# Output weights multiplied by their gates on GpSimd, adaLN products moved ahead of the first QKV, split input wait, sign-turned attention scores

## The chip, the cores and the metric

One core of one Trainium2 chip runs the whole program in one launch. The metric is the device time in microseconds, as the median of runs; lower is better. TensorE (PE) multiplies matrices into eight PSUM banks, VectorE (DVE), ScalarE (ACT) and GpSimd (POOL) do the elementwise work, and DMA queues fed by SyncE (SP) and GpSimd bring the weights from HBM. The engines run their own instruction streams and meet at semaphores.

## The reference

The input is x of 256 rows and 1024 columns, in float32. A first block (gated delta net and dilated attention, then a gated FFN, then a norm) is followed by a second block of two layers. What is changed lies in that second block and at the very start:

```python
for i in range(2):
    mod = silu(c) @ ada_w[i] + ada_b[i]
    sh1, sc1, g1, sh2, sc2, g2 = split(mod, 6)
    h = rms_norm(x, norm_mix_g[i]) * (1.0 + sc1) + sh1
    y = (diff_attention, chunked_attention)[i](h, ...)   # ends in  o @ w_o
    x = x + g1 * y
    h = rms_norm(x, norm_ffn_g[i]) * (1.0 + sc2) + sh2
    x = x + g2 * grouped_moe(h, ...)                     # 16 experts, top 2
```

Both attentions add a bias to the scores and take a softmax: `s = q @ k + bias`, `p = exp(s - max(s))`. The gate g1 is one number for each of the 1024 columns of x, so `g1 * (o @ w_o)` is also `o @ (w_o * g1)`.

## The kernel before

**Products.** A float32 product is made of three fast ones: each weight unit of 128x1024 is split by ScalarE into a high part (`split_hi`, L592) and by VectorE into the rest (`split_lo`, L596), and the activations likewise (`turn_hi`, `turn_lo`, `shift_hi`, `shift_dve`). Raw units come by SyncE into a ring of six (`wraw`), 512 KB each; a slot is free for the next load when VectorE has split it. Units are numbered through the program: QKV of layer l from `U_QKV[l]`, 24 of them, and the output weights w_o from `U_WO[l]`, 8. The w_o units have split buffers of their own (`wtail`, three deep).

**Stages.** The input norm waits for all of x, then QKV, attention and delta net of the first block, the FFN (22 steps of three units), and for each layer of the second block: norm, turn (transposes on TensorE that apply the row's norm factor), QKV in six column groups, attention, output projection (`square`), norm with the router, and the MoE of eight expert pairs, 12 loads of 1 MB each.

**Adaptive modulation.** The vectors `mod` come from 48 bundles of weights (1 MB each, GpSimd's DMA queue, `load_ada`), each used in four narrow TensorE products (`ada_bundle`, L542). `ADA_PLACE` says into which free buffer a bundle is loaded, `ADA_QKV` how many bundles are done after each unit of the first QKV. `ada(n)` makes TensorE do the bundles up to n. Eight bundles (40 to 47) are left for the first QKV. GpSimd spreads the gate rows over the partitions into `mrow` (`mod_spread`).

**Filler.** `busy(bank, n)` (L1176) makes n products that nobody reads. It is called before the turn ahead of each QKV (`BUSY_MOD`, 11), after each output projection (`BUSY_WO`, 8), and in the router (15 and 6).

**Attention.** For each head (and each of two maps in layer 0) VectorE adds the bias to the scores in PSUM and takes the largest (L1021, L1023), then writes its negative (L1026), and ScalarE exponentiates with that as bias (L980).

**End of the output projection.** `add_gated` (L2767, L2770) multiplies each of the four PSUM banks by the gate into hn and adds that to x. TensorE transposes x in four banks (L775); VectorE copies banks 0 and 1 (L2897), ScalarE banks 2 and 3 (L2448) for the router's products (L2176), and VectorE copies their strips (L2901). The FFN's output is added without a gate (`add_to_x`, L2756).

**GpSimd's other work here.** It masks the bias (L1789) once the bias rows have come, and in layer 0 sums squares of the first six heads (L1798, L1800, L1802).

## Time and profile before

| | us |
|---|---|
| median of 3 runs | 1170.31 |
| lowest, highest | 1169.86, 1174.2 |
| the profiled execution | 1173.19 |
| its span on the core | 1171.4 |

The page gives the busy share of each engine, then the span in 40 slices with TensorE's granted clock and the DMA rate. The chain of waits goes back from the last instruction to what released each step. A timeline row has the start, the duration, the engine and line, output and inputs, and in brackets the idle time before it and who ended it. All durations below are of the one profiled execution.

### The profile page before, as it was taken

The numbers are of one execution on the slowest core, as the hardware profiler recorded it, in microseconds if no ns is written. First come the engines' busy times: TensorE is split into PE (matmuls) and PEld (weight loads), VectorE is DVE, ScalarE is ACT, GpSimd is POOL, SyncE is SP. The second block draws the span as 40 slices with busy tenths as digits, with TensorE's granted clock in tenths as the row PEclk, the third lists the DMA queues.
The fourth block names the chain that finished last, engine by engine and source line by source line (L and its number), as shares of the span: only waits on it lengthen the run. The fifth ranks groups of instructions, "written<-read, shape, count | busy, mean of one in ns | idle before, by whom it ended". The sixth has DMA issues, their size and how long they took to land.

```text
span 1171.4 us, 17269 instructions
## 1 busy us (share of the span) xinstructions
PE 1101.8 (94%) x6800; PEld 742.4 (63%) x6800; DVE 611.2 (52%) x1198; ACT 425.5 (36%) x733; POOL 94.9 (8%) x189
## 2 busy tenths in 40 slices
PE   6999899999999999989999999888999999999986
PEld 6887567899999877777634434227878754343422
DVE  3488756767878666586323233226757522332223
ACT  5445433644545454474411102005547421110100
POOL 0211123010211111030000000002000000000000
PEclk9999999999999999999999999998999999999999
DMA  9987694997999858744799999996576669999996
GB/s 278 298 243 274 221 323 138 265 328 221 344 337 284 274 194 309 253 181 170 283 411 410 408 409 409 409 402 204 175 260 234 248 258 409 409 409 409 410 409 252
DMA packets 164719, 356.15 MB, mean 304 GB/s; under 512 B 10648, under 2 KB 79512, under 8 KB 164512
## 3 DMA queue, kind: packets, MB, share of 16 engines
q1 hardware_dynamic: 147600, 295.81, 69.7%
q0 software_dynamic: 17024, 59.26, 14.7%
q8 instruction: 51, 0.84, 0.3%
q14 instruction: 28, 0.23, 0.0%
q10 hardware_dynamic: 16, 0.02, 0.0%
HBM read 351.89 MB, written 7.36 MB: 307 GB/s over the span
## 4 chain that ended last, share of the span: by engine, by line
PE 71%; DMA 14%; DVE 9%; ACT 3%; issue 1%; SPq 1%; POOL 0%; DVEq 0%; ACTq 0%; POOLq 0%
PE bank L606 38%; PE bank L1199 12%; DMA work<-in_moe_w_up 6%; PE bank L1209 6%; DMA ering<-in_moe_w_up 3%; DMA ering<-in_moe_w_gate 3%; PE bank L1168 2%; PE bank L542 2%; PE bank L773 2%; DMA ering<-in_ada_w 1%; DVE wlo L596 1%; PE bank L907 1%; SPq L1700 1%; PE bank L1969 1%; PE bank L1176 1%
## 5 line engine op out<-in xcount | busy, mean ns | idle before, releaser
L596 DVE TENSOR_TENSOR wlo<-wraw,whi 128x1024 fp32r<-128x1024 f32 x150 | 179.0, 1220 | 59.2 <-ACT whi L592 58.7
L592 ACT ACTIVATE whi<-wraw 128x1024 fp32r<-128x1024 f32 x150 | 153.8, 1052 | 56.9 <-PE bank L606 52.7
L606 PE MATMUL bank<-a_hi,whi 128*128 128x256 f32 x512 | 146.2, 286 | 0.3 <-DVE wlo L596 0.3
L606 PE MATMUL bank<-a_lo,whi 128*128 128x256 f32 x512 | 144.8, 283 | 0.0
L606 PE MATMUL bank<-a_hi,wlo 128*128 128x256 f32 x512 | 144.8, 283 | 0.0
L1199 PE MATMUL bank<-ering,work 128*64 128x512 f32 x576 | 129.6, 595 | 9.4 <-DMA ering<-in_moe_w_up 5.0
L1446 DVE TENSOR_TENSOR work<-work,bank 128x512 f32<-128x512 f32 x16 | 11.0, 687 | 205.3 <-PE bank L1199 205.3
L1335 ACT ACTIVATE o_hi<-work 128x512 fp32r<-128x512 f32 x32 | 20.2, 631 | 235.6 <-DVE work L1395 235.3
L606 PE MATMUL bank<-whi,a_hi 128*128 128x512 f32 x256 | 103.9, 406 | 0.8 <-DVE wlo L596 0.8
L606 PEld LDWEIGHTS bank<-a_hi,whi 128*128 128x128 f32 x512 | 98.1, 192 | 9.1 <-issue 7.0
L1199 PEld LDWEIGHTS bank<-ering,work 128*64 128x64 f32 x576 | 40.1, 137 | 96.8 <-issue 77.4
L606 PE MATMUL bank<-whi,a_lo 128*128 128x512 f32 x256 | 99.9, 390 | 0.0
L606 PE MATMUL bank<-wlo,a_hi 128*128 128x512 f32 x256 | 99.9, 390 | 0.0
L606 PEld LDWEIGHTS bank<-a_lo,whi 128*128 128x128 f32 x512 | 98.1, 192 | 0.7
L606 PEld LDWEIGHTS bank<-a_hi,wlo 128*128 128x128 f32 x512 | 98.1, 192 | 0.0
L1395 DVE SCALAR_TENSOR_TENSOR work<-bank,sm,mrow 128x512 f32<-128x512 f32 x32 | 22.7, 747 | 87.6 <-PE bank L1209 87.6
L1209 PE MATMUL bank<-ering,work 128*64 128x512 f32 x288 | 64.2, 595 | 1.1 <-DVE work L1449 1.1
L606 PEld LDWEIGHTS bank<-whi,a_hi 128*128 128x128 f32 x256 | 48.1, 188 | 17.2 <-issue 5.6
L1323 ACT ACTIVATE work<-bank,mcol 128x256 f32<-128x256 f32 x64 | 31.6, 561 | 67.0 <-PE bank L1168 67.0
L606 PEld LDWEIGHTS bank<-whi,a_lo 128*128 128x128 f32 x256 | 48.1, 188 | 10.3
L606 PEld LDWEIGHTS bank<-wlo,a_hi 128*128 128x128 f32 x256 | 48.2, 188 | 9.0 <-issue 0.2
L1199 PE MATMUL bank<-work 128*64 128x512 f32 x192 | 44.3, 596 | 3.7 <-DMA work<-in_moe_w_up 3.7
(332 smaller groups left out, 1877.2 us busy)
## 6 DMA issues: line engine op xcount, KB each, us to landing
ering<-in_moe_w_up SPq DMA_DIRECT2D x36, 1024.0 KB, 18.1
ering<-in_moe_w_down SPq DMA_DIRECT2D x36, 1024.0 KB, 18.1
ering<-in_moe_w_gate SPq DMA_DIRECT2D x36, 1024.0 KB, 17.2
work<-in_ada_w POOLq DMA_DIRECT2D x46, 512.0 KB, 7.0
ering<-in_ada_w POOLq DMA_DIRECT2D x38, 512.0 KB, 5.2
wraw<-in_w_in SPq DMA_DIRECT2D x28, 512.0 KB, 7.0
wraw<-in_a_w_qkv SPq DMA_DIRECT2D x24, 512.0 KB, 5.0
work<-in_moe_w_down SPq DMA_DIRECT2D x12, 1024.0 KB, 18.7
```

The lines of the kernel that those rows point to most:

```text
L542: mm = nc.tensor.matmul(psum[ADA_BANK[g]][32 * q:32 * q + 32, :], silc[:, k, :], ada_part(n, q // 2)[:, (q % 2) * HALF:(q % 2 + 1) * HALF] ...
L592: nc.scalar.activation(w_hi(c), wraw[:, c % RING, :], ACT.Copy).then_inc(w_hi_done, 1)
L596: nc.vector.tensor_tensor(w_lo(u[0]), wraw[:, u[0] % RING, :], w_hi(u[0]).bitcast(F32), ALU.subtract).then_inc(w_lo_done, 1)
L606: mm = nc.tensor.matmul(out_ap, l, r, start=first and n == 0, stop=last and n == len(terms) - 1)
L773: tr = nc.tensor.matmul(dst, v, hn[:, t, 0:P], start=True, stop=True)
L907: mm = nc.tensor.matmul(bank[:, t * P:t * P + (t + 1) * P], q, k, start=True, stop=True)
L1168: mm = nc.tensor.matmul(bank[:, kk * S:kk * S + cols], part[:, t, pair_cols(2 * b + kk)], sel[:, t, 0:cols // PAIR_SLOTS, :], start=n == 1 ...
L1199: mm = nc.tensor.matmul(bank[rows, :], x_e[:, k, rows], eunit(r, e)[:, kk * HALF:(kk + 1) * HALF], start=first and kk == 0, stop=last and ...
L1209: mm = nc.tensor.matmul(psum[4 + half][rows, :], hid_t[:, m % 4, rows], eunit(r, e)[:, half * HALF:(half + 1) * HALF], start=first, stop=last)
L1323: ins = nc.scalar.activation(xe[:, :, k, :], gather_bank(g, b)[:, kk * S:(kk + 1) * S].rearrange("p (a c) -> p a c", a=2), ACT.Identity, b ...
L1335: nc.scalar.activation(o_hi[:, cols], o_f[:, cols], ACT.Copy).then_inc(e_o_hi, 1)
L1395: return nc.vector.scalar_tensor_tensor(out=o_f[:, cols], in0=psum[4 + half][:, :], scalar=sm[:, M_GS:M_GS + 1], in1=mrow[:, 1, cols], op0 ...
```

## The change

1. Each half of x signals a semaphore of its own (`x_rows` and `t5_out`), and the first norm's square of a half waits for that half alone. Later waits on `t5_out` count one more signal.
2. `gate_units` is new: GpSimd multiplies each raw w_o unit in `wraw` by the gate row in `mrow`, 16 units in all. `split_hi` of a w_o unit waits for that multiply, not for the load.
3. `add_gated` is gone; `add_to_x` adds the banks to x. VectorE now makes three of the four copies behind it, ScalarE one. `BUSY_WO` is 3, not 8.
4. `BUSY_MOD` is gone in both layers. In layer 0 bundles 40 to 42 stand in its place, loaded into the buffers of a_hi and a_lo (places 14, 15) and place 13; `ADA_QKV` spreads the remaining five. The bundles accumulate in bank 7, so the fourth group of that turn uses bank 4, once VectorE has read it.
5. In the attentions of the second block the stored scores have their sign turned, so the smallest is the negated largest, and the small negation is gone; ScalarE waits for `sc_read` and multiplies by -1.

```diff
-BUSY_WO = 8
-BUSY_MOD = 11
+BUSY_WO = 3
...
-ADA_TAIL = [0, 1, 2, 0, 1, 2, 11, 12, 13, 16, 2, 13, 16, 2, 13, 16]
+ADA_TAIL = [0, 1, 2, 0, 1, 2, 11, 12, 14, 15, 13, 16, 2, 13, 16, 2]
-ADA_NORM, ADA_LASTS, ADA_FFN = 35, 37, 40
+ADA_NORM, ADA_LASTS, ADA_FFN, ADA_MOD = 35, 37, 40, 43
-ADA_QKV = [40, 40, 40, 41, 41, 42, 42, 43, 43, 44, 44, 45, 45, 46, 46, 47, 47, 48, 48, 48]
+ADA_QKV = [43, 43, 43, 43, 44, 44, 44, 45, 45, 45, 46, 46, 46, 47, 47, 47, 48, 48, 48, 48]
...
+        def gate_units(pool, l, part):
+            for k in part:
+                c = U_WO[l] + k
+                raw = wraw[:, c % RING, :]
+                pool.wait_ge(raw_in[c % RING], 16 * (c // RING + 1))
+                nc.gpsimd.tensor_tensor(raw, raw, mrow[:, 0, :], ALU.mult).then_inc(sub_done, 1)
...
+            if k is not None:
+                act.wait_ge(sub_done, gated_unit(c))
...
-                    act.wait_ge(x_rows, 16 * T)
+                    act.wait_ge((x_rows, t5_out)[t], 16)
...
+                if turn == 3 and b == 3:
+                    pe.wait_ge(full_done, 1)
...
-                        nc.vector.tensor_tensor_reduce(s[:, 0:P], bank[:, 0:P], bias[:, P:S], 1.0, -3e38, ALU.add,
-                                                       ALU.max, sm[:, mx:mx + 1])
+                        nc.vector.tensor_tensor_reduce(s[:, 0:P], bank[:, 0:P], bias[:, P:S], -1.0, 3e38, ALU.add,
+                                                       ALU.min, sm[:, nm_:nm_ + 1])
...
-            for n in range(ADA_NORM + 3, ADA_FFN + 1):
+            for n in range(ADA_NORM + 3, ADA_FFN):
+                load_ada(pool, n)
+
+            pool.wait_ge(w_used, up_unit(U_FFN, FF_STEPS - 1) + 1)
+            for n in range(ADA_FFN, ADA_MOD):
                 load_ada(pool, n)
...
             toe_mask(0)
+            pool.wait_ge(mod_rows, 256)
+            gate_units(pool, 0, range(RING))
...
+            gate_units(pool, 0, range(RING, KC))
...
             toe_mask(1)
+            pool.wait_ge(mod_rows, 512)
+            gate_units(pool, 1, range(KC))
...
-                busy(psum[4], BUSY_MOD)
+                if l == 0:
+                    ada(ADA_MOD)
...
-                for b in (2, 3):
-                    act.wait_ge(tr_done, 4 * (5 + 3 * l) + b + 1)
-                    nc.scalar.activation(full[:, 2 * b:2 * b + 2, :], turn_bank(5 + 3 * l, b)[:, :].rearrange(
-                        "p (k n) -> p k n", k=2), ACT.Copy).then_inc(rt_full_a, 1)
+                act.wait_ge(tr_done, 4 * (5 + 3 * l) + 4)
+                nc.scalar.activation(full[:, 6:8, :], turn_bank(5 + 3 * l, 3)[:, :].rearrange(
+                    "p (k n) -> p k n", k=2), ACT.Copy).then_inc(rt_full_a, 1)
...
-                add_gated(U_WO[l] + 8, 0, l)
-                for b in range(2):
+                add_to_x(U_WO[l] + 8, 2 + l)
+                dve.wait_ge(mod_rows, 256 * (l + 1))
+                for b in range(3):
```

On TensorE, between the last FFN product and the turn of layer 0 (`work` in L542 is a bundle's weights, `con` in L1176 the filler's operand, L773 the turn), there stood:

```order
L542 MATMUL bank2<-work_77,silc_73 32x512 [waits ada_in4]
L542 MATMUL bank2<-work_77,silc_73 32x512 x3
L1176 MATMUL bank4<-con_68 128x128 [waits x_done]
L1176 MATMUL bank4<-con_68 128x128 x10
L773 MATMUL bank4<-hn_67,x_res_66 128x128 [waits hn_done]
L773 MATMUL bank4<-hn_67,x_res_66 128x128 x3
```

and there stands now (the line numbers are those of the changed kernel):

```order
L541 MATMUL bank2<-work_77,silc_73 32x512 [waits ada_in4]
L541 MATMUL bank2<-work_77,silc_73 32x512 x3
L541 MATMUL bank7<-a_raw0_55,silc_73 32x512 [waits ada_in0,x_done]
L541 MATMUL bank7<-a_raw0_55,silc_73 32x512 x3
L541 MATMUL bank7<-a_raw1_56,silc_73 32x512 [waits ada_in1]
L541 MATMUL bank7<-a_raw1_56,silc_73 32x512 x3
L541 MATMUL bank7<-work_77,silc_73 32x512 [waits ada_in5]
L541 MATMUL bank7<-work_77,silc_73 32x512 x3
L793 MATMUL bank4<-hn_67,x_res_66 128x128 [waits hn_done]
L793 MATMUL bank4<-hn_67,x_res_66 128x128 x3
```

The filler is gone, and three bundles stand in its place, each behind the load of its own weights (`ada_in`).

On VectorE, at the end of layer 0's output projection (`wtail` are the last splits, `bank4` to `bank7` the product), there stood:

```order
L596 TENSOR_TENSOR wtail_78<-wraw_49,wtail_78 128x1024 [waits w_hi_done] x6
L2767 TENSOR_TENSOR hn_67<-bank4,mrow_71 128x512 [waits rows_half,mod_rows]
L2770 TENSOR_TENSOR x_res_66<-x_res_66,hn_67 128x512 [waits x_tmp]
L2767 TENSOR_TENSOR hn_67<-bank5,mrow_71 128x512
L2770 TENSOR_TENSOR x_res_66<-x_res_66,hn_67 128x512 [waits x_tmp]
L2767 TENSOR_TENSOR hn_67<-bank6,mrow_71 128x512 [waits rows_half]
L2770 TENSOR_TENSOR x_res_66<-x_res_66,hn_67 128x512 [waits x_tmp]
L2767 TENSOR_TENSOR hn_67<-bank7,mrow_71 128x512 [waits w_used]
L2770 TENSOR_TENSOR x_res_66<-x_res_66,hn_67 128x512 [waits x_tmp]
L2897 COPY work_77<-bank0 128x512 [waits tr_done]
L2897 COPY work_77<-bank1 128x512 [waits tr_done]
L729 RECIPROCAL sm_76<-sm_76 128x2 [waits nrm_rs]
```

and there stands now:

```order
L614 TENSOR_TENSOR wtail_78<-wraw_49,wtail_78 128x1024 [waits w_hi_done] x6
L2787 TENSOR_TENSOR x_res_66<-x_res_66,bank4 128x512 [waits rows_half]
L2787 TENSOR_TENSOR x_res_66<-x_res_66,bank5 128x512
L2787 TENSOR_TENSOR x_res_66<-x_res_66,bank6 128x512 [waits rows_half]
L2787 TENSOR_TENSOR x_res_66<-x_res_66,bank7 128x512 [waits w_used]
L2915 COPY work_77<-bank0 128x512 [waits tr_done,mod_rows]
L2915 COPY work_77<-bank1 128x512 [waits tr_done]
L2915 COPY work_77<-bank2 128x512 [waits tr_done]
L747 RECIPROCAL sm_76<-sm_76 128x2 [waits nrm_rs]
L2919 COPY work_77<-bank4 128x256 [waits rt_ps,nrm_inv]
```

Four adds stand where four multiplies and four adds stood, and a third copy has come.

On GpSimd, between the last bundle loads of layer 0 and the first head's squares, there stood:

```order
L530 DMA hn_67<-in_ada_w_2 128x1024 [waits ada_used]
L530 DMA hn_67<-in_ada_w_2 128x1024
L1789 MEMSET work_77 64x8x64 [waits toe_in]
L1798 ISA
L1798 TENSOR_TENSOR work_77<-hn_67 128x256 [waits att_y]
L1800 TENSOR_TENSOR work_77<-work_77 128x128 [waits sub_done]
L1802 TENSOR_TENSOR work_77<-work_77 128x64 [waits sub_done]
```

and there stands now:

```order
L529 DMA work_77<-in_ada_w_2 128x1024
L1814 MEMSET work_77 64x8x64 [waits toe_in]
L578 ISA
L578 TENSOR_TENSOR wraw_49<-wraw_49,mrow_71 128x1024 [waits raw_in0,mod_rows]
L578 TENSOR_TENSOR wraw_49<-wraw_49,mrow_71 128x1024 [waits raw_in1]
L578 TENSOR_TENSOR wraw_49<-wraw_49,mrow_71 128x1024 [waits raw_in2]
L578 TENSOR_TENSOR wraw_49<-wraw_49,mrow_71 128x1024 [waits raw_in3]
L578 TENSOR_TENSOR wraw_49<-wraw_49,mrow_71 128x1024 [waits raw_in4]
L578 TENSOR_TENSOR wraw_49<-wraw_49,mrow_71 128x1024 [waits raw_in5]
L1825 TENSOR_TENSOR work_77<-hn_67 128x256 [waits att_y]
L1827 TENSOR_TENSOR work_77<-work_77 128x128 [waits sub_done]
```

Six multiplies of raw w_o units stand between the mask and the first head's squares, each behind the load of its unit. Two more stand behind the sixth head's sums, and eight behind the mask of layer 1.

## Rows read from the trace of the kernel before

**Rows 1.** The page, parts 1 and 2: busy time by engine; clock in 40 slices.
```profile
PE 1101.8 (94%) x6800; PEld 742.4 (63%) x6800; DVE 611.2 (52%) x1198; ACT 425.5 (36%) x733; POOL 94.9 (8%) x189
PEclk9999999999999999999999999998999999999999
```

**Rows 2.** Loads of x (both halves), then the first timeline row of ACT.
```profile
DMA to landing us min/median/max: 3.8/4.2/4.6
...
5.84 1.06 ACT L711 ACTIVATE hn<-x_res 128x1024 f32<-128x1024 f32 x1 [3.58 <-DMA x_res<-in_x]
```

**Rows 3.** Chain of waits: start, duration, what. One bundle inside the first QKV.
```profile
435.03 0.99 PE bank L542 x8
```

**Rows 4.** Timeline (start, duration, engine, line, what), end of FFN to first QKV.
```profile
407.05 1.06 POOL L530 DMA_DIRECT2D work<-in_ada_w  x2 [7.14 <-PE bank L2096]
...
413.65 2.72 PE L1176 MATMUL bank<-con 128*128 128x128 f32 x22
...
418.65 5.47 PE L773 MATMUL bank<-hn,x_res 128*128 128x128 f32 x32 [2.28 <-DVE hn L737]
```

**Rows 5.** Busy time by stretch: PE, PEld, DVE, ACT, POOL, clock, DMA share, GB/s.
```profile
407.00:413.00 6.00, 6.00 (x44) 2.98 (x40) 2.48 (x4) 2.83 (x5) 1.06 (x2) 1.00 0.98 377
413.00:418.00 5.00, 3.37 (x30) 2.53 (x22) 2.73 (x4) 3.31 (x9) 0.00 (x0) 1.00 0.04 15
572.00:577.00 5.00, 5.00 (x32) 3.56 (x33) 0.00 (x0) 3.56 (x8) 0.00 (x0) 0.93 0.00 0
600.00:770.00 170.00, 161.44 (x788) 66.27 (x784) 47.57 (x83) 23.96 (x44) 0.00 (x0) 1.00 1.03 409
```

**Rows 6.** Timeline of DVE in layer 0's attention.
```profile
517.85 0.42 DVE L1023 CUSTOM_DVE_ANT_0 work<-bank,work 128x256 f32<-128x256 f32 x1
...
518.43 0.29 DVE L1021 CUSTOM_DVE_ANT_0 work<-bank,work 128x128 f32<-128x128 f32 x1
```

**Rows 7.** Chain of waits at the end of that attention.
```profile
522.79 0.90 PE bank L938 x3
```

**Rows 8.** Timelines around the end of the output projections, both layers.
```profile
409.66 2.48 DVE L2756 TENSOR_TENSOR x_res<-x_res,bank 128x512 f32<-128x512 f32 x4 [2.86 <-PE bank L606]
...
552.45 0.69 DVE L2767 TENSOR_TENSOR hn<-bank,mrow 128x512 f32<-128x512 f32 x1 [4.69 <-PE bank L606]
...
556.57 2.56 PE L775 MATMUL bank<-con,x_res 128*128 128x128 f32 x16 [1.05 <-DVE x_res L2770]
...
559.26 1.06 ACT L2448 ACTIVATE work<-bank 128x512 f32<-128x512 f32 x2
...
561.54 0.42 DVE L2901 COPY work<-bank 128x256 f32<-128x256 f32 x1 [1.98 <-PE bank L2176]
...
934.56 0.43 DVE L2901 COPY work<-bank 128x256 f32<-128x256 f32 x1 [1.98 <-PE bank L2176]
```

**Rows 9.** Timeline between the first MoE and the second QKV.
```profile
795.95 5.06 PE L1176 MATMUL bank<-con 128*128 128x128 f32 x22 [3.45 <-issue]
...
796.86 0.48 DVE L737 TENSOR_SCALAR hn<-con,sm 128x128 f32<-128x128 f32 x2
...
800.81 4.02 PE L773 MATMUL bank<-hn,x_res 128*128 128x128 f32 x32
```

**Rows 10.** Timelines: GpSimd, then DVE, ACT and PE rows that bear on it.
```profile
507.07 0.61 POOL L1798 TENSOR_TENSOR work<-hn 128x256 f32<-128x256 f32 x1 [28.25 <-DVE hn L1068]
...
525.02 0.65 POOL L1802 TENSOR_TENSOR work<-work 128x64 f32<-128x64 f32 x1
...
523.67 1.83 DVE L2878 TENSOR_TENSOR hn<-hn,sm 128x512 f32<-128x512 f32 x2
...
530.43 1.29 DVE L2878 TENSOR_TENSOR hn<-hn,sm 128x512 f32<-128x512 f32 x2
...
545.43 1.06 ACT L592 ACTIVATE wtail<-wraw 128x1024 fp32r<-128x1024 f32 x1 [1.74 <-PE bank L606]
...
862.82 1.06 PE L2120 MATMUL bank<-con,work 128*128 128x128 f32 x8 [0.62 <-DVE work L2837]
```

## What I predict, and why

> **What bounds the kernel now.** I read the busy shares first, then the chain of waits, then the timeline around each place where the chain leaves TensorE. TensorE is busy 94% of the span and its clock stands at 0.9 or more of full in all but one slice [rows 1]. So an edit pays where it takes work off TensorE, or where it shortens a stretch in which TensorE waits or burns filler. The exception is the two MoE stages: from 600 to 770 us the DMA engines are busy without a break at 409 GB/s while TensorE is at 161 of 170 us [rows 5]. There the weight stream sets the pace. But it stands still for 572 to 577 us (share 0.00 in rows 5), just before the first expert product frees a buffer, so a MoE stage ends a fixed time after that first release, and time saved before it is passed on, as long as less than about 5 us is saved between the issue of the first loads and the release. Five places are touched, and I take them in the order of the program.
>
> **1. The start.** The first norm waits for the whole of x. The two halves take 3.8 and 4.6 us to land, and ScalarE's first square starts at 5.84 and lasts 1.06 [rows 2]. So the second was issued at about 1.2, the first some 0.4 before it at 0.8. With a wait of its own, the first square starts at about 0.8 + 3.8 = 4.6 us and is over at 5.7, just before the second half. One square of two leaves the chain: gain 1.05. The raw weights of unit 0 could be late instead; then nothing is gained. Ends 0 and 1.1; I take 1.05, since TensorE runs without a gap once it starts its units.
>
> **2. Three bundles out of the first QKV.** One bundle (eight matmul records) costs 0.99 us in the middle of TensorE-bound products [rows 3]. Before, eight stood there; after, five. Gain 3 x 0.99 = 3.0. They go where 11 filler matmuls (22 records, 2.72 us from 413.65) ran; TensorE then waits until 418.65 for the norm [rows 4]. So 5.0 us are free and 3.0 are wanted, if the weights are there. They are not all: GpSimd issues its last loads before this point at 407.05 [rows 4], the DMA engines are full (share 0.98) from 407 to 413 and idle (0.04) after [rows 5]. The old kernel loads one of the three there, the new one all three, into places that are free by then, but behind ring waits that end at about 407 to 408. Two more bundles than before are 2 x 1.05 MB, at 377 to 409 GB/s 5.1 to 5.6 us behind a queue that ended at 413.3: the last lands near 418.7, its products end near 419.7, and the turn starts 1.0 us late. Cost 1.0. Ends: 1.5, if the issues slip; below nothing, because the turn's 32 transposes ran 5.47 us here, partly at half clock, and 4.02 us in the second layer [rows 4, 9]: if the clock now stays up, 1.4 comes back. I take the cost of 1.0, since three bundles with gaps fill this stretch no better than the filler did. The fourth transpose group now waits for VectorE's first copy; that comes within the second group, so nothing.
>
> **3. Scores with the sign turned.** VectorE's small negation goes, 32 of them. Between the start of one map's second half and the next map's first stand 0.58 us [rows 6], and that half lasts 0.42: so about 0.16 per map. Most of it is hidden, since TensorE works through last_units, transposes and values until the eighth head comes near. Only the last maps of layer 0's attention lie on the chain, which is on VectorE until 522.79 [rows 7]: four maps, 4 x 0.16 = 0.6. If VectorE set the pace for all 16 maps it would be 2.6. In layer 1's attention TensorE has no gap until the last pair; I take 0.2 (0 to 0.5). ScalarE's wait moves from one semaphore to an earlier one, and nothing is queued behind it that runs later.
>
> **4. Gates folded into the weights, twice.** After the last output product VectorE makes eight operations, from 552.45, each 0.69 long and overlapping a little (0.67 apart): the last add ends at 552.45 + 7 x 0.67 + 0.69 = 557.8. TensorE's 16 transposes start at 556.57, ScalarE's two copies run from 559.26 to 560.32, and the strip copy comes at 561.54 [rows 8]. After, there are four adds. In the FFN the same four take 2.48 us, 0.62 each [rows 8]. Two start at 552.45, the third when its product piece is done, about 553.7, and the last ends at 554.9. TensorE may turn from 554.4 on; the 2.56 us of the row bound the 16 transposes, so they end at 556.95 at the latest. ScalarE has only the fourth copy, 0.53, at 557.5, and VectorE's three, which follow the banks as they come, are done earlier. The filler of 3 matmuls, 3/11 of 2.72 = 0.7 us after 553.6, ends at 554.3 and holds nobody up. The last copy moves from 560.32 to 557.5: gain 2.8, and everything to the first expert product moves with it. The second layer repeats the rows 373.02 us later (561.54 and 934.56 in rows 8): 2.8 again. Ends 2.3 and 3.3 each.
>
> What is added is 16 multiplies of 128x1024 on GpSimd. None is in the trace. The nearest row is 128x256 in 0.61 us [rows 10]: four times that is 2.44. The other end is the 128x64 that took 0.65 beside VectorE [rows 10], sixteen times: 10.4. I take 2.44, from the row nearest in shape. Then the multiplies are hidden: eight take 19.5 us, and in the second layer they have from 862.82, when the masks are in, to ScalarE's last split, 545.43 + 373.02 = 918.45 [rows 10]. The last two units wait for their loads, but 2.4 us is less than the time between two splits there, and three split units lie ahead. The price that is not hidden is paid by VectorE: the same pair of multiplies took 1.83 us with GpSimd at work and 1.29 without [rows 10]. Most splits have slack, but before 862.82 TensorE waits 0.62 us for VectorE [rows 10], right where the first multiplies of layer 1 fall. I take 0.5 (0 to 2).
>
> The Trainium skill speaks against this edit (GPSIMD Engine Reference, Elementwise — side-by-side cycle accounting): two-input operations cost GpSimd about 2.6 cycles an element, twice VectorE's time. As an estimate from that page a unit takes 2.2 us; the sum would be the same, since either value is hidden. Its Key points say that GpSimd shares its SBUF interfaces with VectorE, with contention for instructions with two SBUF inputs; the 1.83 against 1.29 us agree.
>
> **5. The filler before the second QKV.** At 795.95 TensorE starts 11 fillers at half clock, 5.06 us, and the turn starts at 800.81 though its input was ready at 797.34 (796.86 + 0.48) [rows 9]. So here the filler is in the way by 3.4 us. Without it the turn starts at about 797.5, but cold. Cold, a record of this kind takes 5.06 / 22 = 0.23 us against 2.72 / 22 = 0.12 [rows 4, 9], and 32 take 7.4 instead of 4.02. If the clock rises on the way, as in layer 0 (5.47), the first product comes 3.4 - 1.4 = 2.0 sooner; if it doesn't, 3.4 - 3.4 = 0. I take 1.4, nearer to layer 0, since that row is a turn that began cold (0 to 2.4).
>
> By the Trainium skill (TensorE: Matmul & The Clock Gate, What's actually happening) the engine's default state is throttled and activity releases it, so filler should pay. The row speaks against it here: the filler itself ran cold and longer than the wait it was to cover. By the page alone this term would be 0.
>
> **The sum.** 1.05 + 3.0 - 1.0 + 0.6 + 2.8 + 1.4 - 0.5 + 0.2 + 2.8 = 10.35 us. The profiled execution took 1173.19 us (span 1171.4) and would take 1162.8; it was 2.9 above the median of 1170.31, so against the median I say 1170.31 - 10.35 = **1160.0 us**.
>
> **Rivals.**
> - *The clock falls where filler is gone.* With 3 fillers instead of 8 the router's transposes and strip products might run cold. Here all were at full clock. Cold, 16 transposes cost 16 x 0.11 = 1.8 us more and the strip products, which lie half beside the copies, about 0.7, twice: 5.0 in all, gain 5.3, 1165.0. Against it: the gap they have to bridge shrinks too, by 2 us.
> - *VectorE sets more of the pace than I think, and the clock stays up in the first turn.* Then 1.4 + 1.0 come back there and 2.0 more in layer 0's attention: gain some 14.5, 1155.8.
> - *The weight stream swallows the router's gain.* If the first sixteen loads were still on the way when the expert products start, both 2.8 would go: gain 4.75, 1165.6. Against it stand the 5 us of idle DMA [rows 5].
> - *GpSimd becomes the bound of the output projection* (slower than before). From 862.82 to 918.45 there are 55.6 us for eight multiplies, so it decides from 6.95 us each. At the upper end of 10.4 they take 83.2, late by 27.6, and about the same in layer 0: 2 x 27.6 - 10.35 = 44.9 us more, 1215. For it: small operations doubled in time beside VectorE. Against: the larger the shape, the less per column (0.65 for 64 columns, 0.61 for 256).
> - *The edit doesn't do what it says*, in that the fold only swaps VectorE's wait for another, is ruled out by the order: four adds stand where eight operations stood, with the same two release points.
>
> **How the numbers follow.** Forecast case 0.66 (gains of 7 to 13.5, so 1156.8 to 1163.3), more gain 0.12, clock 0.12, stream 0.05, GpSimd 0.05. For 8 in 10 I go from 1155.5 to 1165.3: that takes in the better case's centre and the clock rival's, and leaves out the stream's, GpSimd's and the tails. 0.5% is 5.85 us, about what a measurement of this kernel can tell from no change; the line is 1164.5. Faster: 0.66 + 0.12 + half of the clock rival = 0.84. Same: the other half and the stream, 0.11. Slower: 0.05.
>
> **What would show it.** The first a_hi products about 1 us sooner. Five bundle groups in the first QKV, and the turn before it starting 1 us later relative to the FFN's last product; if the last bundle waits for DMA until more than 2 us after the norm, step 2 is wrong. The last copy before the strip products 3.9 us after the last output product instead of 6.7. GpSimd's multiplies at 2 to 3 us; over 7 makes the whole forecast wrong. The second turn starting right after its norm, at clock 0.5, and lasting 5.5 to 6.8. Splits on VectorE of about 1.7 us, not 1.22, beside GpSimd. DMA idle still before the first expert product, some 2 us shorter. A router stage at clock 0.5 would make the clock rival true.

## The result, and the profile after

The changed kernel takes 1176.44 us in the median of six runs (1173.86 to 1177.82), beside 1170.19 for the kernel before: ratio 1.0044, 95% interval 1.0029 to 1.0058. A second set of six gave 1176.25 and a ratio of 1.0066 (1.0044 to 1.0089). So it is 5 to 8 us slower, where I had said 10.35 faster. The profiled execution of the changed kernel took 1176.52 (span 1174.7), that of before 1173.19 (span 1171.4), itself 3 above its median; the traces are therefore only 3.3 us apart.

The page of the changed kernel, parts 1 and 2, against [rows 1]:

```profile
PE 1096.9 (93%) x6736; PEld 736.2 (63%) x6736; DVE 620.5 (53%) x1160; ACT 424.4 (36%) x731; POOL 135.6 (12%) x205
...
PEclk9999999999999999998999999998989999999999
```

TensorE has 64 records less and is busy 5 us less, and the span is longer: it waits more. VectorE has 38 operations less and is busy 9 us more. That is the clue: fewer operations, each longer. And the clock row has three digits under 9 instead of one.

The start of the same operation in both traces, as after minus before, tells where time goes. A stage's share is the change from one row to the next.

| place | before | after | after - before |
|---|---|---|---|
| first transposes on TensorE | 9.32 | 7.89 | -1.43 |
| adds at the FFN's end (VectorE) | 409.66 | 408.56 | -1.10 |
| first product of the first QKV | 423.88 | 424.41 | +0.53 |
| last transposes of that QKV | 490.63 | 490.55 | -0.08 |
| transposes behind the attention | 526.23 | 526.05 | -0.18 |
| adds behind the output projection | 552.45 | 556.89 | +4.44 |
| strip copy in the router | 561.54 | 562.86 | +1.32 |
| norm factors before the second turn (VectorE) | 796.86 | 798.61 | +1.75 |
| transposes of the second turn | 800.81 | 799.24 | -1.57 |
| first product of the second QKV | 804.83 | 804.54 | -0.29 |
| output weights in layer 1, third unit | 909.79 | 916.46 | +6.67 |
| strip copy in the second router | 934.56 | 938.10 | +3.54 |
| end | 1171.4 | 1174.7 | +3.3 |

Most gains are there: both routers won 3.1, the second turn 3.3 less 1.3 given back, the start 1.1. Three stretches lose, and all lie where GpSimd multiplies. The first is the end of the first QKV. From the first product to the last transposes it takes 66.75 us in the kernel before, 63.28 with the bundles moved and no fold (before + bundles and fillers, below), and 66.14 here: 2.9 lost. The second is the first output projection (4.6 lost), the third layer 1 from its last QKV products on (6.95 lost): 14.5 in all.

A fourth loss is hidden behind a row that looks even. With the scores' sign turned, the stretch from those last transposes to the ones behind the attention takes 33.85 us in two traces without multiplies on GpSimd, 35.60 before and 35.50 here. TensorE's clock was at 0.60 from 492 to 496, behind its wait for the blocked VectorE; in the second trace of the changed kernel it stayed at 1.00 there and the stretch took 33.86. So this 1.65 varies from run to run.

**Layer 1, about 860 us.** The changed kernel's timelines of GpSimd, VectorE and TensorE (start, duration, engine, line; in brackets the idle time before and who ended it):

```profile
860.83 14.13 POOL L578 TENSOR_TENSOR wraw<-wraw,mrow 128x1024 f32<-128x1024 f32 x6 [1.77 <-DMA wraw<-in_b_w_o]
...
863.34 1.41 DVE L2854 TENSOR_SCALAR work<-bank,vec 128x512 f32<-128x512 f32 x2 [0.92 <-PE bank L2151]
865.36 0.17 DVE L2805 COPY sm<-bank 128x16 f32<-128x16 f32 x1 [0.62 <-PE bank L2115]
865.46 9.98 DVE L2807 TENSOR_SCALAR swg<-sw,mcol 128x32 f32<-128x32 f32 x8
...
876.59 1.65 PE L927 MATMUL bank<-work 64*128 64x128 f32 x8 [4.63 <-DVE sm L1044]
```

The same eight small operations in the kernel before:

```profile
865.71 1.25 DVE L2790 TENSOR_SCALAR swg<-sw,mcol 128x32 f32<-128x32 f32 x8
```

The row of the group by its own durations, in the changed kernel (min, median, max in ns):

```profile
L2807 DVE TENSOR_SCALAR swg<-sw,mcol x8: 228/1305/2432, 865.5 to 875.2; 128x32 f32<-128x32 f32 x8
```

An operation of 0.23 us took up to 2.43, and 14.13 / 6 = 2.36 is the length of one multiply. Four of the eight lasted as long as a multiply, the last four 0.23, since GpSimd had ended at 874.96. Right before, VectorE's shift of 128x512 out of PSUM ran beside the same multiplies in 1.41 for two, as in the kernel before (1.40). So this isn't a general slowdown. One of the two engines stands still for the whole of the other's instruction, and only where VectorE takes its data from SBUF (and not always there: some operations with one input from SBUF kept their times, see the end). The Trainium skill has this rule (SBUF — State Buffer, Who interferes with whom): the pair of ports that the two share is an exclusive lock, taken by VectorE's instructions with two SBUF inputs or in a mode that uses both ports, and "the other **fully blocks** (not throttle)". The traces agree, with 2.43 for 0.23.

**Layer 0.** VectorE and GpSimd at the end of the first QKV, then in the output projection, with TensorE's wait:

```profile
478.85 5.75 POOL L578 TENSOR_TENSOR wraw<-wraw,mrow 128x1024 f32<-128x1024 f32 x2 [0.84 <-DMA wraw<-in_a_w_o]
...
478.94 3.39 DVE L2875 TENSOR_TENSOR work<-work,sm 128x1024 f32<-128x1024 f32 x1
482.25 6.83 DVE L614 TENSOR_TENSOR wlo<-wraw,whi 128x1024 fp32r<-128x1024 f32 x4
...
536.16 2.37 POOL L578 TENSOR_TENSOR wraw<-wraw,mrow 128x1024 f32<-128x1024 f32 x1 [1.29 <-DMA wraw<-in_a_w_o]
...
536.64 5.24 DVE L614 TENSOR_TENSOR wtail<-wraw,wtail 128x1024 fp32r<-128x1024 f32 x3
...
539.76 1.19 PE L624 MATMUL bank<-wtail,a_hi 128*128 128x512 f32 x2 [2.54 <-DVE wtail L614]
```

In the kernel before, VectorE's multiply at 478.94 took 1.23 and the four splits behind it 4.63. Each engine blocks the other in turn: 3.39 is 2.4 of waiting and 1.0 to 1.2 of work. At 539.76 TensorE had waited 2.54 for one blocked split, and its next pairs of products take 1.19 and 1.05 instead of 0.63: the clock had fallen. The stretches around these waits, in the columns of [rows 5]:

```profile
478.00:493.00 15.00, 12.26 (x59) 8.99 (x59) 13.40 (x11) 7.17 (x10) 9.61 (x5) 0.96 0.43 140
536.00:545.00 9.00, 6.46 (x22) 4.86 (x21) 5.87 (x5) 3.14 (x4) 2.37 (x1) 0.81 0.21 81
862.00:882.00 20.00, 14.80 (x75) 11.48 (x76) 14.20 (x28) 2.56 (x6) 12.96 (x6) 0.83 0.42 161
```

In the kernel before TensorE was busy 15.00 of the first 15 us and 19.38 of the last 20, at clock 1.00.

**The places that went as foretold.** The chain behind the first output projection: adds, three copies, the last copy on ScalarE, the strip.

```profile
556.89 2.48 DVE L2787 TENSOR_TENSOR x_res<-x_res,bank 128x512 f32<-128x512 f32 x4 [4.62 <-PE bank L624]
559.69 1.89 DVE L2915 COPY work<-bank 128x512 f32<-128x512 f32 x3 [0.31 <-PE bank L795]
...
561.06 0.60 ACT L2478 ACTIVATE work<-bank 128x512 f32<-128x512 f32 x1 [0.17 <-PE bank L795]
...
562.86 0.42 DVE L2919 COPY work<-bank 128x256 f32<-128x256 f32 x1 [1.22 <-PE bank L2207]
```

From the first add to the strip copy it is 5.97 us, and 9.09 in [rows 8]. The two turns on TensorE, and the bundles before the first:

```profile
414.09 1.06 PE L541 MATMUL bank<-a_raw,silc 128*32 128x512 f32 x8 [1.47 <-DVE x_res L2833]
416.56 1.88 PE L541 MATMUL bank<-a_raw,silc 128*32 128x512 f32 x8 [1.41 <-DMA a_raw<-in_ada_w]
419.12 1.52 PE L541 MATMUL bank<-work,silc 128*32 128x512 f32 x8 [0.68 <-DMA work<-in_ada_w]
420.57 3.84 PE L793 MATMUL bank<-hn,x_res 128*128 128x128 f32 x32
...
799.24 5.31 PE L793 MATMUL bank<-hn,x_res 128*128 128x128 f32 x32 [4.98 <-DVE hn L755]
```

### The profile page after: what moved, and what is told of

Read it like the earlier page. It is cut to its first block, busy times and chain, and to the rows that moved or that the text cites. A ratio compares the mean times of both kernels' runs of the same rounds, so it can differ in the third digit from the quotient of the medians.

```text
span 1174.7 us, 17124 instructions
## 1 busy us (share of the span) xinstructions
PE 1096.9 (93%) x6736; PEld 736.2 (63%) x6736; DVE 620.5 (53%) x1160; ACT 424.4 (36%) x731; POOL 135.6 (12%) x205
## 4 chain that ended last, share of the span: by engine, by line
PE 71%; DMA 13%; DVE 10%; ACT 3%; issue 2%; SPq 1%; POOL 0%; DVEq 0%; ACTq 0%; POOLq 0%
PE bank L624 36%; PE bank L1220 13%; PE bank L1230 7%; DMA work<-in_moe_w_up 5%; DMA ering<-in_moe_w_up 3%; PE bank L1189 3%; PE bank L541 2%; PE bank L793 2%; DVE wlo L614 2%; DMA a_raw<-in_moe_w_up 2%; DMA ering<-in_moe_w_gate 1%; DMA ering<-in_ada_w 1%; PE bank L927 1%; DMA work<-in_ada_w 1%; PE bank L1999 1%
## 5 line engine op out<-in xcount | busy, mean ns | idle before, releaser
L614 DVE TENSOR_TENSOR wlo<-wraw,whi 128x1024 fp32r<-128x1024 f32 x150 | 181.4, 1236 | 58.8 <-ACT whi L610 58.0
```

The source lines that it names most:

```text
L614: nc.vector.tensor_tensor(w_lo(u[0]), wraw[:, u[0] % RING, :], w_hi(u[0]).bitcast(F32), ALU.subtract).then_inc(w_lo_done, 1)
```

## The experiments

Each kernel was timed beside runs of the kernel before on the same chip. The last column is the ratio's distance from 1, of 1170.5 us.

| kernel | median us | ratio and interval | us |
|---|---|---|---|
| changed kernel, again | 1176.25 | 1.0066 (1.0044 to 1.0089) | +7.7 |
| before + fold alone | 1173.84 | 1.0028 (1.0013 to 1.0044) | +3.3 |
| layer 0 held back | 1170.04 | 0.9982 (0.9968 to 0.9997) | -2.1 |
| layer 1 held back | 1168.92 | 0.9979 (0.9960 to 0.9998) | -2.5 |
| before + start and sign | 1169.55 | 0.9991 (0.9977 to 1.0005) | -1.1 |
| before + bundles and fillers | 1168.08 | 0.9969 (0.9954 to 0.9983) | -3.6 |
| changed, fold undone | 1167.57 | 0.9973 (0.9960 to 0.9986) | -3.2 |
| held and quarters, with filler | 1168.02 | 0.9981 (0.9966 to 0.9997) | -2.2 |
| held and quarters | 1166.43 | 0.9955 (0.9938 to 0.9972) | -5.3 |
| the same, two bundles | 1164.13 | 0.9939 (0.9916 to 0.9962) | -7.1 |
| all held back | 1163.38 | 0.9934 (0.9919 to 0.9950) | -7.7 |
| quarters | 1161.89 | 0.9930 (0.9906 to 0.9953) | -8.2 |
| held, linked quarters | 1161.87 | 0.9919 (0.9896 to 0.9942) | -9.5 |
| fold on VectorE | 1161.20 | 0.9914 (0.9896 to 0.9933) | -10.1 |
| fold on VectorE, two bundles | 1161.99 | 0.9913 (0.9890 to 0.9937) | -10.2 |
| held, linked, two bundles | 1158.50 | 0.9892 (0.9875 to 0.9909) | -12.6 |
| all held back, two bundles | 1158.47 | 0.9889 (0.9869 to 0.9910) | -13.0 |

### Is it the fold?

The fold undone:

```
-BUSY_WO = 3
+BUSY_WO = 8
...
-            gate_units(pool, 0, range(RING))
...
-                add_to_x(U_WO[l] + 8, 2 + l)
+                add_gated(U_WO[l] + 8, 0, l)
```

> The changed kernel with the fold of the gates undone: no multiplies on GpSimd, eight operations of VectorE after the last output product, 8 fillers and two copies each on VectorE and ScalarE, as before; x halves, bundles and scores as in the changed kernel. Theory A (GpSimd's multiplies block VectorE where TensorE waits for it): what is left is the start -1.1, the bundles -3.0, the late first turn +1.7, attention -0.6 and the second turn -2.1, so 5.1 under the kernel before, 1165. Rival B (the fold is a gain and something else in the change loses): the 6.8 us that the router stages won in the trace go, 1183.

The kernel before with the same lines the other way round, the fold alone:

> The kernel before with only the fold: 16 multiplies on GpSimd, four adds of VectorE, 3 fillers, three copies on VectorE and one on ScalarE. Theory A: the losses read in the changed kernel's trace, 2.7 at the end of the first QKV, 1.2 of clock behind it, 4.4 in the first output projection, 6.7 at the start of the second attention, less 3.2 and 3.6 in the routers: +8.2, 1178. Rival B: faster than before by 5.6, 1164.6.

Measured: -3.2 without the fold, +3.3 with it alone. Rival B falls. Theory A's sizes were off both times. The fold alone costs 3.3, but on top of the other edits 8 to 11 (from -3.2 to +5.1 or +7.7). The trace of the fold alone says why. Layer 0 loses only 0.4 (from -0.82 at the first product of its QKV to -0.44 at the adds behind the output projection), although splits of 3.31 and 3.42 us show that VectorE was blocked there too. Layer 1 loses 6.0, but elsewhere: one split of its QKV took 3.41, and three of the eight small operations were blocked. A collision costs or spares a whole multiply by where GpSimd's work happens to fall, so its price can't be carried from one schedule to another.

### Lock or shared bandwidth?

The multiplies held back in three places, behind the VectorE work that they had met there:

```
             pool.wait_ge(mod_rows, 256)
+            pool.wait_ge(w_lo_done, U_WO[0])
             gate_units(pool, 0, range(RING))
...
+            pool.wait_ge(w_lo_done, U_WO[0] + 5)
             gate_units(pool, 0, range(RING, KC))
...
             pool.wait_ge(mod_rows, 512)
+            pool.wait_ge(sc_read, ATT_M[2] + 1)
             gate_units(pool, 1, range(KC))
```

> The changed kernel with GpSimd's multiplies held back in three places, and nothing left out: the first six of layer 0 until the last split of the first QKV is made, the last two until VectorE has made the fifth split of the output weights, all of layer 1 until the first score of its attention is read (so behind VectorE's eight small router weights). Theory A, in the form of a lock (one of the two engines stands still for the whole of the other's operation): the losses at these three places go, 2.7 + 4.4 + 6.7, less up to 3 that come back elsewhere in layer 0's attention: 1163 to 1166. Rival C (the engines share a bandwidth and both slow down for as long as both work): the multiplies take as much from VectorE wherever they stand, and the gain is under 3: 1174 to 1176.

The multiplies in quarters:

```
-                nc.gpsimd.tensor_tensor(raw, raw, mrow[:, 0, :], ALU.mult).then_inc(sub_done, 1)
+                for q in range(4):
+                    part_ = slice(256 * q, 256 * q + 256)
+                    ins = nc.gpsimd.tensor_tensor(raw[:, part_], raw[:, part_], mrow[:, 0, part_], ALU.mult)
+                ins.then_inc(sub_done, 1)
```

> The changed kernel with each of GpSimd's 16 multiplies of 128x1024 made as four of 128x256 (0.61 us each in the kernel before), same data, same work. Lock: an operation of VectorE waits for at most one piece of 0.6 us, so the eight small router weights of layer 1 take about 5 us instead of 9.98, the blocked splits about 1.8 instead of 3.4, and the kernel comes to 1168 to 1171. Rival C (shared bandwidth): the same bytes take the same time, 1176.

Held: 1163.38, as the lock has it; GpSimd does the same work and 13 us are back. Quarters: 1161.89, 6 under the forecast of 1168 to 1171: against the changed kernel its trace is 4.6 sooner in the output projection and 13.5 at the third unit of layer 1. Some 1.9 of this is not the multiplies: from the router's strip copy to the norm factors before the second turn it took 233.85 us instead of 235.75, with TensorE's clock at 1.00 from 560 to 580, where the changed kernel had 0.91. Where the rest beyond the forecast comes from is open. The group of eight with quarters, then held:

```profile
L2810 DVE TENSOR_SCALAR swg<-sw,mcol x8: 447/776/781, 859.2 to 863.7; 128x32 f32<-128x32 f32 x8
```

```profile
860.24 1.25 DVE L2810 TENSOR_SCALAR swg<-sw,mcol 128x32 f32<-128x32 f32 x8
...
864.72 14.07 POOL L578 TENSOR_TENSOR wraw<-wraw,mrow 128x1024 f32<-128x1024 f32 x6 [11.19 <-DVE sm L1044]
```

With pieces a quarter as long each small operation waits a quarter as long: at most 0.78 instead of 2.43. Sharing would have left the sum as it was (rival C falls). Held, none of the eight waits, and while the attention's score operations read PSUM, the six multiplies run undisturbed, 2.35 each. The hold-backs don't clear every meeting. Two small operations of layer 0's attention took 2.44 each (0.22 and 0.35 alone), and that attention took 35.56 us instead of 33.85.

### Which place?

Layer 1's hold-back alone, then layer 0's two:

> The changed kernel with one edit: GpSimd waits, before the multiplies of layer 1, until the first score of that layer's attention is read, that is behind VectorE's eight small router weights. In the changed kernel's trace these eight took 9.98 us instead of 1.25, the first values came 5.0 later than in the kernel before relative to the QKV and 1.7 more went by a lower clock. Lock theory: 5 to 6.7 faster than the changed kernel, 1170 to 1171.5. If waits on VectorE there are covered (rival): no difference.

> The changed kernel with only the two hold-backs of layer 0 (first six behind the first QKV's splits, last two behind the fifth split of the output weights). Held run less layer 1's share: 13 in all, 6.7 of them in layer 1, so 5 to 6.5 here, 1170 to 1171.5; by the traces 2.9 at the end of the QKV and its clock, 2.0 to 3 in the output projection.

> The changed kernel once more, beside the same runs of the kernel before, for the size of what was to be explained: ratio 1.0044 again, 1176, if the six runs of it were fair; the runs with one edit each (1168.9 and 1170.0) are then 6 to 7 faster than it.

Layer 1's single wait takes the kernel from 1176.3 to 1168.9 (7.3), layer 0's to 1170.0 (6.2), both to 1163.4 (12.9). They nearly add. Layer 1 agrees with the 6.95 of the table of places; layer 0 gets back less than its 2.9 + 4.6, since the held multiplies now meet the attention (37.19 us for it in that trace). The ratios give a wider spread: 7.6 to 10.2 for layer 1, 7.3 to 9.8 for layer 0, 12.9 to 15.4 for both, by which set of the changed kernel is taken. So the multiplies' meetings with VectorE are most of the miss of 15.5 to 18 us, and the held kernel (-7.7) is still 2.7 short of the forecast.

### The fold without GpSimd

```
-                nc.gpsimd.tensor_tensor(raw, raw, mrow[:, 0, :], ALU.mult).then_inc(sub_done, 1)
+                nc.vector.tensor_tensor(raw, raw, mrow[:, 0, :], ALU.mult).then_inc(gt_done, 1)
...
+                gate_units(dve, l, range(3))
                 attention_dve(dve, 1 + l, link, sub_sums if l == 0 else None)
...
+                for k in range(4, KC):
+                    splits(U_WO[l] + k - 1)
+                    gate_units(dve, l, range(k, k + 1))
                 splits(U_WO[l] + 8)
```

> The changed kernel with all 16 multiplies of output weights by gates on VectorE and none on GpSimd: in each layer three before the attention, the others one by one between the splits of the output projection. Same products, same adds, same router. Lock theory: a multiply costs VectorE 1.2 us of its own (a split of that shape takes 1.22) and nobody else anything; three fit in the 4 us in which it waits for the first scores, five in the 1.57 that it has between two splits: the fold's gain stays (3.2 and 3.6 in the two routers) and its loss goes, 1161 to 1164. Rival E (the fold itself is what costs, by the wait of ScalarE's splits for the gated weights): as the changed kernel, 1176. If VectorE has no room before layer 0's attention: up to 3 more, 1167.

Measured 1161.2, inside the forecast, and rival E falls: the splits wait for gated weights here too. Its VectorE, before layer 0's attention and in the output projection:

```profile
488.89 3.48 DVE L572 TENSOR_TENSOR wraw<-wraw,mrow 128x1024 f32<-128x1024 f32 x3
...
536.82 1.22 DVE L572 TENSOR_TENSOR wraw<-wraw,mrow 128x1024 f32<-128x1024 f32 x1
537.96 1.22 DVE L608 TENSOR_TENSOR wtail<-wraw,wtail 128x1024 fp32r<-128x1024 f32 x1
539.09 1.22 DVE L572 TENSOR_TENSOR wraw<-wraw,mrow 128x1024 f32<-128x1024 f32 x1
540.23 1.22 DVE L608 TENSOR_TENSOR wtail<-wraw,wtail 128x1024 fp32r<-128x1024 f32 x1
```

A multiply costs 1.22 here, half of GpSimd's 2.4, in gaps that VectorE had. Against the kernel with the fold undone (0.9973) the fold is then worth 6.9 us (0.9914). The idea of folding the gates was right; the engine was wrong.

### Quarters and hold-backs together

> The three hold-backs and the quarters together, everything else as in the changed kernel. Lock theory: both take away the same waits, so little is added to the better of the two, 1162; the one place that only the hold-backs clear is the end of the first QKV (four splits in 6.47 us with quarters, 4.63 held), up to 1.5: 1160 to 1162.5. If the quarters gained by something other than shorter waits (rival: another chance of the clock, whose low stretch before the second layer's gather is missing in that trace), the combination stands where the held one stood, 1163 to 1165.

Measured 1166.4: slower than either alone, and outside both bounds. Its VectorE and GpSimd at 496 us:

```profile
496.70 7.32 DVE L1072 SCALAR_TENSOR_TENSOR sm<-sm 128x2 f32<-128x2 f32 x1
...
487.36 16.65 POOL L580 TENSOR_TENSOR wraw<-wraw,mrow 128x256 f32<-128x256 f32 x24 [8.14 <-DVE wlo L617]
```

An operation on two columns, 0.22 us elsewhere, stood for 7.32 us, through ten pieces, until GpSimd had no more. With whole multiplies held back it stood for one:

```profile
497.46 2.44 DVE L1069 SCALAR_TENSOR_TENSOR sm<-sm 128x2 f32<-128x2 f32 x1
```

So I let each piece wait for the one before it (a semaphore that the piece counts up and the next waits on), and each unit's first piece for the unit before, with the hold-backs kept:

```
+                if gated_unit(c) > 1:
+                    pool.wait_ge(sub_done, gated_unit(c) - 1)
...
+                    if q:
+                        pool.wait_ge(piece_done, 3 * (KC * l + k) + q)
```

> The combination of hold-backs and quarters, but each quarter waits for the one before it by a semaphore, so that a gap stands between two of them (0.08 us where such a chain stands in the kernel before). Theory F (VectorE's operation starves because GpSimd's next piece is already queued when the pair comes free): no operation of VectorE waits longer than one piece, the 7.3 us at 496.7 become under 1, and the time is 3 under the combination, 1161 to 1163.5. Rival (who gets the pair is chance): some runs of pieces still hold VectorE for several us, 1164 to 1167.

Measured 1161.9, and in its trace the operation takes 0.48:

```profile
494.40 0.48 DVE L1077 SCALAR_TENSOR_TENSOR sm<-sm 128x2 f32<-128x2 f32 x1
494.91 1.22 DVE L1081 SCALAR_TENSOR_TENSOR work<-work,sm 128x128 f32<-128x128 f32 x2
```

The stretch from the QKV's last transposes to those behind the attention took 40.80 us in the combination's trace and 33.94 with the links. Theory F is supported, not shown. The trace with the filler has the same unlinked pieces and its longest wait of this kind is under 1 us, so it doesn't happen each time; in the traces of quarters alone and of the combination with two bundles the operation stood for 3.99 and 6.18. Nor do linked pieces beat whole multiplies where both were held back with two bundles (1158.50 and 1158.47).

### The bundles, the filler, the start and the sign

> The kernel before with only the bundles moved (three before the first QKV's turn, in other places of memory, filler gone there and before the second turn). By the traces: bundles -3.0, turn late by 1.65 net, second turn -2.1: 3.4 faster, 1167.4. By the prediction's terms: -3.0 + 1.0 - 1.4 = -3.4, the same sum. Rival (a cold turn takes the whole gain): within 1 of the kernel before.

> The combination with the 11 fillers before the second layer's turn put back, to price their removal alone. As the prediction had it: 1.4 slower than the combination (0 to 2.4); the changed kernel's trace says 2.1 (3.35 won up to the turn, 1.29 given back in it). Rival (the filler holds the clock): no slower, or faster.

> The kernel before with only the halves of the input waited for apart and the scores stored with their sign turned. By the prediction 1.05 + 0.6 + 0.2 = 1.85 faster; by the difference of two runs (all but the fold -3.2, the bundles alone -3.4) nothing, 0 to 0.5. Trace of the changed kernel: first turn 1.4 sooner, of which 1.1 is left at the end of the FFN.

Bundles and fillers alone: -3.6, forecast -3.4. The filler put back costs 1.6 by the medians and 3.0 by the ratios, with intervals that overlap a little (forecast 1.4). Start and sign: -1.1, with an interval (-2.7 to +0.6) that holds 0 and -1.85 alike.

Two bundles instead of three:

```
-ADA_NORM, ADA_LASTS, ADA_FFN, ADA_MOD = 35, 37, 40, 43
+ADA_NORM, ADA_LASTS, ADA_FFN, ADA_MOD = 35, 37, 40, 42
```

> The combination, but with two bundles instead of three in the gap before the first QKV and the third back among its units. In the traces the third bundle's weights are what the turn waits for last: its products start 1.8 to 2.4 us after the second's end and run at half clock, and the turn begins 3.1 us after its input. Theory D (the third load is what makes the turn late): the turn starts at the end of the second bundle's products or its input, about 2.5 to 3 sooner, the bundle costs 0.99 in the QKV: 1.5 to 2 faster than the combination. Rival: any gap there lets the clock fall, and the turn runs cold either way, then 0 to 1 faster.

> The changed kernel with whole multiplies held back in the three places and two bundles before the first QKV. The held run came to 1163.4, two bundles are worth 2: 1161.4. Against the combination of hold-backs and quarters with two bundles (1164.1): if quarters that follow each other without a gap starve VectorE (its operation of 0.22 us waited 6 and 7 us at 495 to 504 in those traces, 2.4 in the held one), this one is 2 to 4 faster; if that was chance, equal.

> Hold-backs, quarters that wait for each other, and two bundles before the first QKV. Linked quarters with three bundles came to 1161.9, whole multiplies held with three to 1163.4 and with two to 1158.5: two bundles are worth 2 to 5, so 1158 to 1160 if the two savings add; 1161 to 1162 if the gain of two bundles is partly chance of the clock, as it was between the two runs with multiplies on VectorE (1161.2 and 1162.0).

> The same with two bundles instead of three before the first QKV. In the combination this took 2.3 us off (1166.43 to 1164.13), in its trace 4.6 up to the turn, 1.9 given back in it as it ran at half clock, and 0.99 for the bundle: 2 faster than the run with three, 1159 to 1162. If the gain there was chance of the clock: within 1.

Two are better by 1.9, 5.3 and 3.2 in three pairs and by nothing in the fourth (ratios); in the first and third the intervals overlap. The timeline of TensorE held back with two bundles:

```profile
416.67 1.94 PE L541 MATMUL bank<-a_raw,silc 128*32 128x512 f32 x8 [1.52 <-DMA a_raw<-in_ada_w]
418.53 5.75 PE L793 MATMUL bank<-hn,x_res 128*128 128x128 f32 x32
```

The turn starts 2.4 sooner than in the held kernel with three (420.91), but runs at half clock, 5.75. How much is kept depends on where the clock's low stretch falls, which differs from run to run; why the kernel with VectorE's fold gained nothing stays open. The fastest kernels of the study, 1158.5, are 1.1% under the kernel before and 1.5% under the changed one.

## Why the prediction was wrong, step by step

- **Start, 1.05**: right. The first square starts at 4.11 instead of 5.84, and 1.10 is left at the FFN's end.
- **Three bundles, 3.0, late turn, 1.0**: near in sum (1.8 won in this trace, 2.0 forecast), by errors that cancel. Three bundles less took 3.5 off the first QKV (66.75 to 63.28), not 3.0. The last bundle's products began at 419.12, near the forecast load (418.7), but at half clock (1.52 and 1.88 instead of 0.99), so the turn started 3.0 late against the FFN's end, not 1.0. Of that 1.4 came back, since the turn itself then ran at full clock, 3.84; I had that as a way below the bound. In the held kernel the turn took 5.70 (420.91 to 426.61) and nothing came back.
- **Scores, 0.6 and 0.2**: start and sign together measured 1.1 where 1.85 was said, too small to tell by the times. By the traces 0.6 was too little: layer 0's attention took 33.85 us with the sign turned and no multiplies (start and sign alone, and the fold undone), against 35.60, 35.50 and 35.53 in three traces with the old sign. That is 1.7, and most of it is a term that I had not. TensorE's waits for VectorE in the last 19 us of the stretch hardly differ: 3.4 us before, the longest 1.8, and 3.2 with start and sign alone, the longest 1.2. But its clock fell to 0.5 near the end of the stretch in all three traces with the old sign, and stayed at 1.00 in the others.
- **Gates, 2.8 each**: right, 3.12 and 3.13.
- **GpSimd's duration, 2.44**: right (2.35 to 2.40 undisturbed). The rival "GpSimd becomes the bound", at 10.4, was the wrong danger.
- **The price to VectorE, 0.5 (0 to 2)**: this is the step that failed. By the trace it was 14.5 us. I read 1.83 against 1.29 in [rows 10] as a slowdown of some 0.5 beside GpSimd, and looked for a single place without slack. Read as waits, the rows fit better: the two multiplies took 0.96 and 0.94 us, each some 0.27 more than undisturbed, and each ended 0.55 after the end of a short GpSimd operation (524.08 and 524.94). VectorE had waited out what was left of these. A wait of that kind scales with the length of GpSimd's instruction, and I added instructions four times as long: up to 2.4 for each operation of VectorE they meet. I knew of the contention and took its size from the wrong variable. The same holds for the 0.65 us of 128x64, which I took as a price of small operations: by the same reading it was GpSimd's own wait for VectorE (the same shape took 0.32 for each of the five heads before).
- **"Most splits have slack"**: wrong at two places. The blocked splits after 482.25 push back the shifts behind them on VectorE, to 489.01, and TensorE waits 2.7 for these, and the split at 536.64 was the one that TensorE waited for. I also named 862.82, the right place in layer 1, but counted the shift before it and not the eight small operations behind it.
- **The clock**: I had it fall where filler is gone. The routers stayed as they were. It fell behind the new waits (0.81 over 536 to 545, 0.83 over 862 to 882), which is in the 14.5, and in some runs in layer 0's attention.
- **Filler before the second QKV, 1.4**: near; 3.3 won up to the turn and 1.3 given back in it make 2.0, inside 0 to 2.4.
- **The stream**: DMA still idles before the first expert product (share 0.00 at 576 to 578), so the first MoE passes on nearly all (+1.32 in, +1.75 out). Right.

Put together: the traces are 3.3 us apart, and without the three losses they would be 11.2 apart the other way, near the forecast of 10.35. That sum holds the hidden loss in the attention and the larger gain of the sign, which cancel.

## What to carry to other kernels

Before work is moved to GpSimd, list every VectorE operation in the stretch that reads two inputs from SBUF, and every `TENSOR_SCALAR` from SBUF to SBUF, and price each meeting at the full length of GpSimd's instruction, plus the clock that TensorE loses behind the wait. If the work must be on GpSimd, put it where VectorE reads PSUM (scores, shifts out of a bank) and hold it there with a wait; otherwise give VectorE the work when it has gaps, where here it took half as long.

When a row shows an operation a little longer beside another engine, ask first whether it waited for the rest of one instruction: the excess then says nothing on how it grows.

## What the runs showed of the hardware

- VectorE and GpSimd exclude each other for whole instructions: 0.23 became 2.43 beside multiplies of 2.36 and 0.78 beside pieces of 0.7. The blocked ones were operations with two inputs from SBUF (`TENSOR_TENSOR`, `SCALAR_TENSOR_TENSOR`) and `TENSOR_SCALAR` from SBUF to SBUF. A `TENSOR_REDUCE` of 128x1024 (1.22 at 478.08 in the fold alone) and a `RECIPROCAL` of 128x4 (0.18 at 496.49 in the combination) read SBUF beside a multiply and kept their times. Operations of VectorE with PSUM as source (128x512 at 0.74, scores at 0.42) and ScalarE's splits (3.89 for four at 480 us) kept their times.
- A row of GpSimd instructions that are all ready can hold VectorE for longer than one of them: 7.32, 6.18 and 3.99 us in three traces, for an operation of 0.22. With a semaphore between the pieces no operation in that place waited longer than 0.56 us, in two traces.
- A wait costs more than its length when the clock falls behind it: TensorE's 4.63 us at 876 went with a loss of 6.95, and its products behind the 2.54 at 539 took 1.19 for two instead of 0.63, the lower of the two levels, 1.2 instead of 2.4 GHz.
